# Dots that read the tokens' rows from PSUM, low halves by GpSimd in other windows, and gates loaded by eights

## The reference

```python
q = (xt @ wq).reshape(T, PEER_HEADS, 2, PEER_HALF)         # 8 heads, 2 sides
s = jnp.einsum('thpd,hpnd->thpn', q, subkeys)              # 128 keys a side
sv, si = lax.top_k(s, K)                                   # K = 16
comb = (sv[:, :, 0, :, None] + sv[:, :, 1, None, :]).reshape(T, PEER_HEADS, K * K)
cs, ci = lax.top_k(comb, K)
idx = ia * PEER_NKEYS + ib                                 # of 128*128 experts
g = jax.nn.softmax(cs, axis=-1)
a = jnp.einsum('td,thkd->thk', xb, u_tab[eb])
w = gb * jax.nn.gelu(a, approximate=False)
out = jnp.einsum('thk,thkd->td', w, v_tab[eb])
h = _layer_norm(DEEPNORM_ALPHA * h + out + sigmoid(h @ W_g + b_g) * (p @ W_p), g2, b2)
```

## Time and profile before

| | |
|---|---|
| median of 3 runs | 1356.83 us (1353.93 to 1361.5) |
| the profiled execution | 1352.02 us, span 1350.2 us |
| TensorE | 1289.5 us busy, 96% of the span |
| VectorE | 1189.5 us, 88% |
| ScalarE | 665.2 us, 49% |
| GpSimd | 651.4 us, 48% |
| mean granted TensorE clock | 0.986 |
| DMA | 155045 packets, of them 73184 under 2 KB; 405.03 MB, 300 GB/s over the span, about 390 GB/s from 500 us on |

### The profile page before, as it was taken

One profiled execution on the slowest core, in us unless ns is written; L12 is line 12 of the kernel. 1 busy time (PEld: TensorE's weight loads), 2 busy tenths in 40 slices (PEclk: granted clock), 3 DMA queues, 4 the chain that ended last, 5 costly groups with the idle time before them and its releaser, 6 DMA issues.

```text
span 1350.2 us, 22849 instructions
## 1 busy us (share of the span) xinstructions
PE 1289.5 (96%) x7713; PEld 715.7 (53%) x7713; DVE 1189.5 (88%) x2408; ACT 665.2 (49%) x935; POOL 651.4 (48%) x387
## 2 busy tenths in 40 slices
PE   6999999899995999999998999999899999999997
PEld 4554555456663677777764555555344444444444
DVE  8866388899999899999977999888998888898897
ACT  5652645356672777777743343333333333344342
POOL 4741232478771333433454666556665545464402
PEclk9999999899997999999998999999999999999999
DMA  7232421278874799999999999999999999999972
GB/s 294 95 110 67 136 79 63 94 247 284 300 260 150 218 345 386 393 390 392 390 414 353 386 392 391 400 375 385 359 392 391 391 391 390 373 383 385 385 264 107
DMA packets 155045, 405.03 MB, mean 300 GB/s; under 512 B 12512, under 2 KB 73184, under 8 KB 152800
## 3 DMA queue, kind: packets, MB, share of 16 engines
q1 hardware_dynamic: 113504, 253.21, 52.5%
q0 software_dynamic: 41472, 151.01, 28.9%
HBM read 359.09 MB, written 44.56 MB: 299 GB/s over the span
## 4 chain that ended last, share of the span: by engine, by line
PE 43%; DVE 23%; DMA 20%; issue 11%; ACT 2%; SPq 1%; DVEq 0%; ACTq 0%
PE bank L773 10%; PE bank L761 8%; PE bank L762 7%; PE bank L763 7%; DMA area<-gelu_scratch 7%; DMA area<-gates_scratch 6%; DMA raw<-tiles_dram 5%; DVE cut L1448 4%; PE bank L1038 2%; DVE ple_gate L1931 2%; PE bank L788 2%; DVE area L1924 1%; DVE area L1692 1%; DMA gates_scratch<-area 1%; DVE area L1683 1%
## 5 line engine op out<-in xcount | busy, mean ns | idle before, releaser
L773 PE MATMUL bank<-cut,area 128*128 128x512 f16 x2208 | 487.8, 381 | 16.6 <-DVE area L1924 11.3
L761 PE MATMUL bank<-hT,cut 128*128 128x352 f16 (+1 forms) x1216 | 395.1, 325 | 19.8 <-DVE cut L1448 16.1
L762 PE MATMUL bank<-hT,cut 128*128 128x352 f16 (+1 forms) x1216 | 394.6, 324 | 0.0
L763 PE MATMUL bank<-hT,cut 128*128 128x352 f16 (+1 forms) x1216 | 394.4, 324 | 0.0
L1069 ACT ACTIVATE cut<-raw 128x1024 f16<-128x1024 f32 x238 | 249.7, 1055 | 242.2 <-DMA raw<-tiles_dram 212.7
L773 PEld LDWEIGHTS bank<-cut,area 128*128 128x128 f16 x2208 | 215.6, 98 | 280.3 <-DVE area L1924 12.7
L1448 DVE SCALAR_TENSOR_TENSOR cut<-raw,cut 128x1024 f16<-128x1024 f32 x190 | 240.5, 1267 | 42.9 <-ACT cut L1069 42.7
L636 POOL TENSOR_TENSOR cut<-raw,cut 128x1024 f16<-128x1024 f32 x56 | 123.9, 2223 | 106.7 <-DVE pass_word L1698 72.7
L761 PEld LDWEIGHTS bank<-hT,cut 128*128 128x128 f16 x1216 | 119.3, 98 | 99.1 <-DVE cut L1448 16.8
L763 PEld LDWEIGHTS bank<-hT,cut 128*128 128x128 f16 x1216 | 119.4, 98 | 76.3 <-issue 1.4
L644 POOL DMA_INDIRECT ple_sb<-u_rows_dram,expert_id x64 | 102.2, 1597 | 119.0 <-DVE dots L1659 100.8
(11 more groups left out here) (223 smaller groups left out, 1692.7 us busy)
## 6 DMA issues: line engine op xcount, KB each, us to landing
raw<-tiles_dram SPq DMA_DIRECT2D x298, 512.0 KB, 6.6
gates_scratch<-area SPq DMA_DIRECT2D x12, 2048.0 KB, 11.4
area<-gates_scratch SPq DMA_DIRECT2D x32, 768.0 KB, 10.5
gelu_scratch<-gelu_out SPq DMA_DIRECT2D x88, 192.0 KB, 5.4
area<-gelu_scratch SPq DMA_DIRECT2D x22, 768.0 KB, 12.4
norm_rows<-norms_dram SPq DMA_DIRECT2D x3, 1024.0 KB, 8.0
hn<-x_dram SPq DMA_DIRECT2D x4, 512.0 KB, 4.7
out_dram<-hn SPq DMA_DIRECT2D x3, 512.0 KB, 2.7
```

Of the source, the lines that this page charges most:

```text
L761: nc.tensor.matmul(dst, w[0], hT[:, 0, k, 0:width], start=(k == 0), stop=False)
L762: nc.tensor.matmul(dst, w[0], hT[:, 1, k, 0:width], start=False, stop=False)
L763: last = nc.tensor.matmul(dst, w[1], hT[:, 0, k, 0:width], start=False, stop=(k == KD - 1))
L773: mm = nc.tensor.matmul(bank[:, 2 * tt + h, :], lhs(a)[:, tt * P:(tt + 1) * P], cut[:, t.slot, b, h * HALF:(h + 1) * HALF], start=(first a ...
```

## The change

The dots of the selection, of the gate rounds and of the kept tiles read the tokens' rows from PSUM: ScalarE copies `extra_h`, and later the last token tile, into two banks (`probe`). Portions of low halves are let go by `open_window`: window 2u+1 opens in unit u ahead of the dots and the second pass, window 2u+2 at the unit's end, ahead of its last dots and of the next unit's first pass; in a window GpSimd does its lows first and its gathers after. All 32 extra dots now lie in the selection (24 before), 68 instead of 76 in `both`. In the gate rounds GpSimd makes the low half of every second tile, between its gathers, and ScalarE scales these tiles. Gates are loaded for eight experts in two halves of the token groups, 768 KB each in runs of 1 KB, and asked for a group of eight ahead. The two gelu buffers lie over `picked`, so the first two gelu loads wait for `sparse_w` and stand in the last group of `both`.

```diff
 SELECTION = ((0, 1, 0, TT), (1, 2, 2, 2), (3, 2, 2, 2), (5, 2, 2, 2), (7, 1, 2, 2),
              (1, 2, 0, 2), (3, 2, 0, 2), (5, 2, 0, 2), (7, 1, 0, 2))
 LATTER_HALF = 5
-LOWS_IN_PASS = (5, 1, 3, 1, 2, 1, 3, 1, 2, 1, 3, 11, 6, 5, 6, 5, 0, 0)
-DOTS_IN_UNIT = ((0, 0),) * 5 + ((4, 4),) * 3 + ((0, 0),)
-assert len(LOWS_IN_PASS) == 2 * len(SELECTION) == 2 * len(DOTS_IN_UNIT) and sum(LOWS_IN_PASS) == POOL_TILES
+LOWS_IN_WINDOW = (4, 2, 3, 1, 3, 1, 3, 2, 2, 0, 3, 2, 5, 4, 5, 4, 4, 2, 6)
+DOTS_IN_UNIT = ((0, 0),) * 5 + ((0, 6), (2, 6), (2, 6), (2, 8))
+assert len(LOWS_IN_WINDOW) == 2 * len(SELECTION) + 1 and len(DOTS_IN_UNIT) == len(SELECTION) and sum(LOWS_IN_WINDOW) == POOL_TILES
 U_EARLY = U_TOPK + U_SOFTMAX + U_GATES + U_KEPT
 N_BOTH = N_U - U_EARLY
 T_BOTH = T_U + U_EARLY
...
-EIGHT_DOTS = (26, 26, 24)
+EIGHT_DOTS = (23, 23, 22)
 EIGHT_SUMS = (24,)
 LATE_SUMS = (10, 10, 10, 10, 10, 9, 9, 9, 9, 9, 9)
 assert U_GATES + EARLY - EXTRA + KEPT_DOTS + sum(EIGHT_DOTS) == HK and sum(EIGHT_SUMS) + sum(LATE_SUMS) == HK
 assert len(EIGHT_DOTS) + len(EIGHT_SUMS) == EIGHTS and len(LATE_SUMS) + 1 == N_LATE // 8 and N_LATE % 8 == 0
-assert EARLY % EARLY_SLOTS == 0 and (EXTRA - EARLY) % 8 == 0 and EARLY < EXTRA < U_GATES - 8
+assert EARLY % EARLY_SLOTS == 0 and (EXTRA - EARLY) % 8 == 0 and EARLY == EXTRA and U_GATES % 2 == 0
 BATCH = 16
 VG = 4
+GG = 8
 
 
 FINAL_ORDER = (ND, *range(ND))
...
 
+        probe = bank[:, 4:6, :].rearrange("p a n -> p (a n)")
         raw = sb("raw", [P, RING, D])
...
+        gelu_in = part([2, VG, TD])
+        assert taken[0] <= AREA - 2 * D
 
         def halves_of(t):
...
 
-            def load_gates(group, first, parity):
-
-                at_least(sp, weight_done, VG * (group - 1))
-                sp.dma_start(gates_in[:, parity],
-                             gates_dram[:, :, bass.ds(first, VG), :].rearrange("c p e t -> p c e t")
-                             ).then_inc(gates_loaded[parity], 16)
-
-            def load_gelu(group, parity):
-
-                src = gelu_dram[group] if isinstance(group, int) else \
-                    gelu_dram[bass.ds(group, 1)].rearrange("a p e t -> (a p) e t")
-                sp.dma_start(gelu_in[:, parity], src).then_inc(gelu_loaded[parity], 16)
+            def load_gates(group, half):
+
+                first = GG * group + U_EARLY if group < EIGHTS else GG * (group - EIGHTS)
+                chunks = slice(GCH // 2 * half, GCH // 2 * (half + 1))
+                at_least(sp, weight_done, GG * (group - 1))
+                sp.dma_start(gates_in[:, group % 2, chunks],
+                             gates_dram[chunks, :, first:first + GG, :].rearrange("c p e t -> p c e t")
+                             ).then_inc(gates_loaded[group % 2], 16)
+
+            def load_gelu(group):
+
+                at_least(sp, weight_done, N_BOTH + VG * (group - 1))
+                sp.dma_start(gelu_in[:, group % 2], gelu_dram[group]).then_inc(gelu_loaded[group % 2], 16)
 
             def load_norms(stage):
...
                 if c == U_EARLY - U_KEPT + 5:
                     for s in range(2):
                         sp.wait_ge(gates_stored[s], 16 * (GCH // 2))
-                    load_gates(0, U_EARLY, 0)
-            load_gates(1, U_EARLY + VG, 1)
+                    load_gates(0, 0)
+                    load_gates(0, 1)
+            load_gates(1, 0)
             for i in range(2):
                 load(Tile(T_BOTH + i + LOAD_AHEAD))
 
...
-                    t = Tile(T_BOTH + 2 + 16 * e + 2 * p) if isinstance(e, int) else Tile(T_BOTH + 2 + 2 * p, 16, e)
+                    t = Tile(T_BOTH + 2 + 16 * e + 2 * p)
                     if t.c < T_LATE - 2:
                         load(t.plus(LOAD_AHEAD))
                         load(t.plus(1 + LOAD_AHEAD))
-                    if p % 4 == 2:
-                        s = p // 4
-                        if isinstance(e, int) and e == EIGHTS - 1:
-                            load_gates(2 * e + 2 + s, VG * s, s)
-                        else:
-                            load_gates(2 * e + 2 + s, U_EARLY + VG * (2 * e + 2 + s), s)
+                    if e == 0 and p == 0:
+                        load_gates(1, 1)
+                    if p in (5, 7):
+                        load_gates(e + 2, p // 7)
+                    if e == EIGHTS - 1 and p in (1, 3):
+                        sp.wait_ge(sparse_w_done, 1)
+                        load_gelu(p // 2)
 
             for j in range(VG):
                 sp.wait_ge(gelu_stored[j], 16 * STORED)
-            with sp.Fori(0, EIGHTS - 2) as e:
+            for e in range(EIGHTS):
                 both(e)
-            load_gelu(0, 0)
-            load_gelu(1, 1)
-            both(EIGHTS - 2)
-            both(EIGHTS - 1)
             for n in range(T_LATE - 2, T_LATE):
                 load(Tile(n + LOAD_AHEAD))
 
             def late(e):
-                fixed = isinstance(e, int)
                 for j in range(8):
-                    t = Tile(T_LATE + 8 * e + j) if fixed else Tile(T_LATE + j, 8, e)
-                    if not fixed or t.n + LOAD_AHEAD < T_ALL:
+                    t = Tile(T_LATE + 8 * e + j)
+                    if t.n + LOAD_AHEAD < T_ALL:
                         load(t.plus(LOAD_AHEAD))
-                    if j % 4 == 1 and not fixed:
-                        s = j // 4
-                        load_gates(2 * EIGHTS + 2 * e + s + 2, VG * (2 * e + s + 2), s)
-                        load_gelu(2 * e + s + 2, s)
-                    elif j % 4 == 1 and 2 * e + j // 4 + 2 < N_LATE // VG:
-                        s = j // 4
-                        load_gates(2 * EIGHTS + 2 * e + s + 2, VG * (2 * e + s + 2), s)
-
-            with sp.Fori(0, N_LATE // 8 - 2) as e:
+                    if j in (4, 6) and e + 2 < N_LATE // GG:
+                        load_gates(EIGHTS + e + 2, j // 6)
+                    if j % 4 == 1 and 2 * e + j // 4 + 2 < STORED:
+                        load_gelu(2 * e + j // 4 + 2)
+
+            for e in range(N_LATE // 8):
                 late(e)
-            late(N_LATE // 8 - 2)
-            late(N_LATE // 8 - 1)
             sp.wait_ge(rows_used, EXTRA + 2 * HK)
             load_norms(2)
...
 
-            low, begun = POOL_FIRST, 0
-            for n, count in enumerate(LOWS_IN_PASS):
-                gathers = 0
-                if n == 2 * LATTER_HALF:
+            low, begun, dotted = POOL_FIRST, 0, 0
+            for n, count in enumerate(LOWS_IN_WINDOW):
+                if n:
+                    pool.wait_ge(window_open, n + 1)
+                    dotted += DOTS_IN_UNIT[(n - 1) // 2][(n - 1) % 2]
+                for _ in range(count):
+                    pool_low(Tile(low))
+                    low += 1
+                if n >= 2 * LATTER_HALF:
                     pool.wait_ge(ids_done, 1)
-                    gathers = EARLY_SLOTS
-                elif n:
-                    pool.wait_ge(pass_begun, n + 1)
-                    gathers = min(DOTS_IN_UNIT[(n - 1) // 2][(n - 1) % 2], EARLY - begun)
-                for j in range(max(count, gathers)):
-                    if j < gathers:
+                    done = dotted - DOTS_IN_UNIT[(n - 1) // 2][(n - 1) % 2]
+                    for _ in range(begun, min(EARLY, done + EARLY_SLOTS)):
                         gather(begun)
                         begun += 1
-                    if j < count:
-                        pool_low(Tile(low))
-                        low += 1
             assert begun == EARLY and low == POOL_FIRST + POOL_TILES
 
             pool.wait_ge(ids_done, 2)
-            for n in range(EARLY, EXTRA + 2 * HK):
+            for n in range(EARLY, EARLY + ROW_RING):
                 if n == EARLY + FREE_SLOTS:
                     pool.wait_ge(ple_added, ND)
                     pool.wait_ge(gated, TT)
+                gather(n)
+            for pair in range(U_GATES // 2):
+                t = Tile(T_U + U_TOPK + U_SOFTMAX + 2 * pair + 1 + SPLIT_AHEAD)
+                pool.wait_ge(lo_cut, t.n)
+                pool_low(t)
+                for n in range(EARLY + ROW_RING + 2 * pair, EARLY + ROW_RING + 2 * pair + 2):
+                    gather(n)
+            for n in range(EARLY + ROW_RING + U_GATES, EXTRA + 2 * HK):
                 gather(n)
...
 
-            def scale_and_split_hi(t):
+            def scale_and_split_hi(t, later=None):
 
                 act.wait_ge(tile_in[t.slot], 16 * (t.round + 1))
                 nc.scalar.activation(raw[:, t.slot, :], raw[:, t.slot, :], ACT.Copy,
                                      scale=S_W).then_inc(raw_scaled, 1)
-                act.wait_ge(raw_scaled, t.n - POOL_FIRST + 1)
+                act.wait_ge(raw_scaled, t.n - POOL_FIRST + 1 if later is None else POOL_TILES + later + 1)
                 act.wait_ge(tile_used, t.n - RING + 1)
                 nc.scalar.activation(cut[:, t.slot, 0, :], raw[:, t.slot, :], ACT.Copy).then_inc(hi_cut, 1)
...
 
+            act.wait_ge(extra_h_in, 16 * (P // TOK))
```

(55 more changed lines are left out.)

41 lines of the change are left out of this document (13 added, 28 removed).

## The result

| | before | after |
|---|---|---|
| median | 1355.38 us (1351.58 to 1361.5) | 1335.33 us (1335.05 to 1335.88) |
| ratio | | 0.9865, 95% interval 0.9833 to 0.9897 |
| profiled execution, span | 1352.02, 1350.2 us | 1335.88, 1334.1 us |

The changed kernel is 1.35% faster, 18 us by the ratio (the two medians lie 20 us apart); the forecast was 1333. Between the two profiled executions there are 16.1 us, and four moments say where they are: the first mask of the gate rounds, TensorE's first matmul of a weighted v tile, the start of the late stage (in every kernel taken at the same v tile, the one behind the stall), the end of its v tiles. The last border is good to some 0.4 us.

The account below looks back on a forecast made before the run. TensorE, busy nearly throughout, was taken as the bound, so gains are its stalls and the half clock after them. Terms 13 + 2.5 - 2 + 5 + 5 = 23.5 us gave 1328.5 profiled, 1333 as median; range 1315 to 1350.

Parts of the forecast that it names:

- PSUM dots: Selection and gate rounds: dots reading one operand from PSUM are not stretched by GpSimd's lows, 1.15 to 1.2 us each.
- rival 3: Dots from PSUM are held up by lows like those from SBUF; selection +9 us, pairs 10.03, time 1382; chance 0.06.
- E and A: TensorE's losses at 239 to 253 and 416.4 us, in the selection: 23.2 us before, 10 after, gain 13.
- rival 1: All cover holds and rows come in time; the selection gains 19 us, the time is 1322; chance 0.17.
- Gate rounds: 460 to 678 us: GpSimd takes half of each pair's low, TensorE becomes the bound, gain 2.5 us.
- First gates: Before the first weights, 716 to 731 us: make_weight(0) waits for 1.57 MB instead of 0.79, costing 2 us.
- B: TensorE's loss at 945 to 960 us, stage with both: of 7 us, 5 taken back by the new loads.
- Late: Late stage, 1040 to 1200 us: half the gates packets and a longer lead take back 5 of 6 us.
- From profile to median: End of the sum: the median lay 4.8 us above the profiled execution, so 1328.5 profiled became 1333.

Follow-up runs that it names:

- the run: Changed kernel, but in the gate rounds VectorE makes both low halves of a pair in one instruction and GpSimd none: 1339.75 us, ratio 0.9896.
- alone: The kernel before with only the part on gates (loads by eights a group ahead, gelu loads unrolled with their wait): 1348.78 us, ratio 0.9961.
- short runs: Changed kernel, but each gates load brings four experts of all chunks, in runs of 512 bytes instead of 1 KB: 1344.18 us, ratio 0.9928.

## Why the prediction was right, and where not

The range and the sign held, and most mechanisms of the forecast are those of the trace. The number came closer than its terms, by luck:

- **PSUM dots.** Right: 1.22 us beside a low half, none stretched, and with them rival 3 fell. The run with dots from SBUF bears out its price in the gate rounds, a pair at 9.93 (forecast 10.03), but not in the selection: its first mask comes 26 us later than before, where that rival had 9, and the time is 1394 us (forecast 1382). The rule of the Trainium skill, SBUF, State Buffer, "Who interferes with whom", agrees: 3.12 with two SBUF inputs, 1.22 with one. For one SBUF input the page says so only outside VectorE's 2-port modes, a limit that the forecast left out; a cast and a shift with one SBUF input each were stretched to 6.85 us (before) and 4.84 us (changed). In which mode they ran no run here shows.
- **E and A, forecast 13, measured 7.0.** The mechanism was seen (gathers behind lows, and a stall at the softmax tiles, forecast 5, measured 3.7), the size was off: idle 12.8 us in five places instead of some 7 in two or three. Dots wait 1.4, 1.5 and 15.1 us in windows 14, 16 and 18, not 3 to 4 in each, and 3.0 in window 17; and one shift beside low halves took 4.84 us, where the forecast had about 2 us in each of 3 to 4 units. Missed was that gathers, asked for last in a window, also run into the next window and hold up its lows. Rows asked for one window earlier give 10 to 11 us back: the first mask then comes 18.8 us earlier than before, and rival 1, where rows come in time, had 19.
- **Gate rounds, 2.5.** Measured 3.2 us on TensorE's stretch (210.7 to 207.5) and 4.2 by the run; the masks' pace alone, 24*(9.06-8.78) = 6.7, overstates it. Right in size, but the forecast put GpSimd's low half beside the two dots; it runs into the mask behind them (a low half from 493.26 to 495.40, the mask from 494.29), which is stretched to 3.27 us. VectorE's new idle time covers that.
- **First gates, -2.** Measured -0.9 here and -2.1 alone; the load took 22.34 instead of 19.33, and here the store ahead of it 13.95 instead of 16.41.
- **B, +5, measured -2.1: the step that failed.** Its text weighed SyncE's wait on sparse_w_done and the bytes, and passed over the other wait in the same load, for weights that VectorE makes later than SyncE comes there, with four tile loads behind. That wait held the tile loads back for 14 us and TensorE for 9.08. Without it the time falls by 5.5 us, and the stage with both takes 6.6 us less than before, near the forecast's 5; the bytes that it weighed then cost 4.7 in the late stage.
- **Late, +5, measured 5.8**, but the reason was half wrong: the packets gave all of it, and the lead, which did end VectorE's waits for loads, gave no time (shown with short runs only). The same packets gave 3.1 us in the rest, which the forecast left out: with short runs the last raw tiles come late, and TensorE waits there 2.3 us before, 3.5 with short runs and not at all in the changed kernel.
- **From profile to median.** The sum is 7.4 us short of the 23.5. That the time is only 2 us off is luck, since two misses of opposite sign meet, the 7.4 us and the 4.8 us added for the median: the profiled execution of the changed kernel lay 0.5 above its median, not 4.8 below. As a difference the forecast was 23.8 us, and 18 to 20 were measured.

## What to carry to other kernels

When a wait is added to a queue issued in program order, find the step at which each engine comes to it, for every semaphore it names, and count what stands behind; a wait for a buffer that nothing has used yet holds back the queue like a real one (5.5 us here). When work is put ahead of requests for data on the same engine, ask for the data a turn earlier, or the freed time becomes a wait for it. Where a stage runs at what memory gives, longer runs of a transfer can be worth more than an earlier issue (8.5 us against nothing here).
